# Two blocks on one core: projections of two pairs of heads moved beside linear and sparse attention, and another order of the first block's modulation

## The reference

```
mod_lat = silu(c) @ w_ada[l] + b_ada[l]          # 6 * 1024 columns, also for the context
h = rms_norm(x, g_mix) * (1 + sc1) + sh1
x = x + gt1 * mixer(h);  x = x + gt2 * conv_ffn(rms_norm(x, g_ffn) * (1 + sc2) + sh2)
```

```
h = rms_norm(x);  proj = h @ w_in   # qa ka va | qi ki wi | qb kb vb rb gl | uc
qa, ka, qi, ki = partial_rope(...)
o_a = sparse attention: per query the 128 best keys by the index scores, 8 heads of 64
o_b = gated linear attention of 4 heads, normalised, times silu(rb)
o_c = multi-scale pooling of uc
x = x + concat(o_a, o_b, o_c) @ w_out;  x = x + conv_glu_ffn(rms_norm(x))
```

## Time and profile before

| | us |
|---|---|
| median of 3 runs | 3632.78 (3628.01 to 3633.86) |
| profiled execution | 3633.83, its span 3632.0 |
| PE busy | 3459.5 (95%) |
| DVE busy | 2102.3 (58%) |
| ACT busy | 1321.1 (36%) |
| POOL busy | 121.8 (3%) |

### The profile page before, as it was taken

The page is one execution under the profiler, slowest core; times in us unless marked ns, Lnnn a source line. Parts: engine busy times, 40 slices in busy tenths (PEclk is TensorE's granted clock), DMA queues, the critical chain, the costliest instruction groups (busy, mean ns, idle before and its releaser), DMA issues.

```text
span 3632.0 us, 45947 instructions
## 1 busy us (share of the span) xinstructions
PE 3459.5 (95%) x18168; PEld 2771.1 (76%) x18168; DVE 2102.3 (58%) x3295; ACT 1321.1 (36%) x2084; POOL 121.8 (3%) x70
## 2 busy tenths in 40 slices
PE   6999999989999989999998999998999999899998
PEld 4866778878888877667777888775788877578887
DVE  4854663455575575445546664694566449646643
ACT  3344353333213323444433333344323234532322
POOL 0000000000000000000000000240000006000000
PEclk9999999999999999999999999998999999889999
DMA  5410202212261232101132333220232332013332
GB/s 231 150 41 13 86 25 87 64 49 62 99 220 60 96 124 69 41 18 47 54 95 78 93 95 104 91 83 7 83 96 93 102 99 82 30 58 97 94 98 93
DMA packets 79221, 300.56 MB, mean 83 GB/s; under 512 B 8784, under 2 KB 8912, under 8 KB 77904
## 3 DMA queue, kind: packets, MB, share of 16 engines
q1 hardware_dynamic: 77760, 291.47, 25.3%
q10 hardware_dynamic: 1296, 6.82, 0.5%
HBM read 296.16 MB, written 2.10 MB: 82 GB/s over the span
## 4 chain that ended last, share of the span: by engine, by line
PE 82%; DVE 11%; ACT 3%; DMA 2%; issue 2%; SPq 0%; DVEq 0%; ACTq 0%
PE ps L651 22%; PE ps L653 22%; PE ps L652 22%; PE ps L969 2%; DVE work L2716 2%; DVE top L2715 2%; PE ps L1011 2%; PE ps L1016 1%; PE ps L1039 1%; PE ps L1025 1%; PE ps L1046 1%; DVE ps L2187 1%; DVE ada_o L2187 1%; PE ps L706 1%; ACT split L1421 1%
## 5 line engine op out<-in xcount | busy, mean ns | idle before, releaser
L2009 DVE TENSOR_TENSOR split<-raw,split 128x1024 fp32r<-128x1024 f32 x412 | 504.4, 1224 | 821.6 <-ACT split L1421 820.7
L1421 ACT ACTIVATE split<-raw 128x1024 fp32r<-128x1024 f32 x442 | 466.5, 1056 | 756.3 <-PE ps L653 670.0
L651 PE MATMUL ps<-h,split 128*128 128x512 f32 x1328 | 532.5, 401 | 9.3 <-DVE split L2009 5.7
L653 PE MATMUL ps<-h,split 128*128 128x512 f32 x1328 | 525.3, 396 | 0.0
L652 PE MATMUL ps<-h,split 128*128 128x512 f32 x1328 | 525.2, 396 | 0.0
L651 PE MATMUL ps<-h_hl,split 128*128 128x512 f32 (+1 forms) x776 | 296.3, 382 | 19.3 <-DVE h_hl L2081 13.8
L651 PEld LDWEIGHTS ps<-h,split 128*128 128x128 f32 x1328 | 250.8, 189 | 75.8 <-issue 8.9
L652 PEld LDWEIGHTS ps<-h,split 128*128 128x128 f32 x1328 | 250.8, 189 | 60.7 <-issue 2.9
L653 PEld LDWEIGHTS ps<-h,split 128*128 128x128 f32 x1328 | 250.6, 189 | 59.4
L653 PE MATMUL ps<-h_hl,split 128*128 128x512 f32 (+1 forms) x776 | 279.4, 360 | 0.0
L652 PE MATMUL ps<-h_hl,split 128*128 128x512 f32 (+1 forms) x776 | 279.0, 359 | 0.0
(11 more groups left out here) (408 smaller groups left out, 6305.3 us busy)
## 6 DMA issues: line engine op xcount, KB each, us to landing
raw<-wstream SPq DMA_DIRECT2D x442, 512.0 KB, 3.5
ada_t<-ada_w SPq DMA_DIRECT2D x80, 512.0 KB, 4.8
first_w<-ada_first SPq DMA_DIRECT2D x4, 2048.0 KB, 25.6
x<-x_in SPq DMA_DIRECT2D x1, 3072.0 KB, 13.4
x<-x_in ACTq DMA_DIRECT2D x1, 3072.0 KB, 11.0
ada_c<-c_in SPq DMA_DIRECT2D x2, 1024.0 KB, 4.9
out<-x SPq DMA_DIRECT2D x8, 256.0 KB, 2.2
par<-params SPq DMA_DIRECT2D x1, 1345.0 KB, 6.6
```

The costliest lines, as they stand in the source:

```text
L651: nc.tensor.matmul(o, wh, a[0], start=first, stop=False)
L653: return nc.tensor.matmul(o, wl, a[0], start=False, stop=last)
L1421: nc.scalar.activation(split[:, n % SPLIT_SLOTS, 0, :], raw[:, n % RAW_SLOTS, :], copy).then_inc(hi_split, 1)
L2009: nc.vector.tensor_tensor(split[:, n % SPLIT_SLOTS, 1, :], raw[:, n % RAW_SLOTS, :], split[:, n % SPLIT_SLOTS, 0, :].bitcast(F32), ALU.sub ...
```

## The change

*First block.* PE's order at the start becomes modulation 0, sums of the norm, pick 0, modulation 2, spread, pick 2, modulation 1; modulation 3 comes before chunk 1, pick 1 before chunk 2, pick 3 before chunk 3. The two tiles of `ADA_AFTER[10]` are reduced before the low part of slab 10 instead of behind it. In both down projections the tiles are dealt over seven splits instead of nine, with the bias and the gains behind the eighth slab closed.

*Second block.* The slabs' order becomes qa 0, ka 0, qa 1, ka 1, ... Only pairs 0 and 1 are projected in `in2`; two decays go behind the first projection and one behind each of the next three events, and DVE makes two `decayed` behind the first rope and one behind each other. qa 2 is projected between `products(0)` and `products(1)`, ka 2 behind `products(1)`, both in bank 6. qa 3 and ka 3 are projected in bank 7 in pieces of one chunk (three matmuls) beside steps 0 to 7 of `dsa`, in two places of a step, before the values and before the transposes; their rotations stand in steps 4 and 8. All value tiles go to the two halves of bank 6. `mix` is eight buffers instead of one, since its old place is that of the activations `h2`, which now live on.

```diff
+ADA_AHEAD = LORA_SLABS + H_B
...
+IN2_ROPED = roped([((name, m), LAT, True) for m in range(2) for name in ("qa", "ka")])
+INDEX_ROTS, IN2_ROTS = 3, 3 + 4
+LATE_PAIR, LAST_PAIR = 2, 3
+
+def late_pieces(i):
+    if i < 4:
+        return [[("gemm", ("qa", LAST_PAIR), 2 * i)], [("gemm", ("qa", LAST_PAIR), 2 * i + 1)]]
+    if i == 4:
+        return [[("rot", ("qa", LAST_PAIR), 0)], [("gemm", ("ka", LAST_PAIR), 0), ("gemm", ("ka", LAST_PAIR), 1)]]
+    if i < 8:
+        return [[("gemm", ("ka", LAST_PAIR), 2 * i - 8)], [("gemm", ("ka", LAST_PAIR), 2 * i - 7)]]
+    return [[("rot", ("ka", LAST_PAIR), 0)] if i == 8 else [], []]
...
@@ SP, loads of tiles
-                        upto = ADA_SLOTS[group] + tiles * max(g - ahead - RAW_SLOTS, 0) // (BOTH_DOWN - 2)
+                        upto = ADA_SLOTS[group] + tiles * max(g - ahead - RAW_SLOTS, 0) // (BOTH_DOWN - 4)
@@ PE, first_two and mla(0)
+                    if 1 <= k <= len(beside):
+                        beside[k - 1]()
...
                     modulation(0)
                     tiles = norm_sums([(DC, BOTH)], sumN)
+                    pick(0)
                     modulation(2)
-                    pick(0)
                     norm_spread(0, tiles)
                     pick(2)
-                    beside = (lambda: (modulation(1), modulation(3)), lambda: (pick(1), pick(3)))
+                    modulation(1)
+                    beside = (lambda: modulation(3), lambda: pick(1), lambda: pick(3))
@@ PE, gla
                 products(0)
+                gemm(open_slab(), 0, DC, whole, (0, SEQ), True, bank=6)
                 pe.wait_ge(att_off, pairs.now() + 1)
                 pe.wait_ge(att_masked, pairs.now() + 1)
                 products(1)
                 pairs.add(2)
+                rotate("perm_2", qa[:, LATE_PAIR, :], owner[6], bank=7)
+                gemm(open_slab(), 0, DC, whole, (0, SEQ), True, bank=6)
@@ PE, dsa
+                rotate("perm_2", ka[:, LATE_PAIR, :], owner[6], bank=7)
...
                     if i + 2 < n:
                         scores(i + 2)
+                    if i == 0:
+                        pe.wait_ge(o_taken, outs.now())
+                    fill(i, 0)
                     if i:
                         value(i - 1)
+                    fill(i, 1)
                     turn_maps(i)
@@ ACT
-                projections(IN2_ROPED, INDEX_ROTS, beside=lambda j: decays(j - INDEX_ROTS))
+                projections(IN2_ROPED, INDEX_ROTS, beside=((0, 1), (2,), (3,), (4,)))
...
+                    for kind, name in late_ends(i):
+                        late_rot() if kind == "rot" else late_tile(name)
                     act.wait_ge(t_ready, items.now() + i + 1)
@@ DVE, split_low
+                    if n == ADA_AHEAD:
+                        ada_tiles(1, sum(ADA_AFTER[j] for j in ADA_AFTER if j < n), ADA_AFTER[n])
                     dve.wait_ge(hi_split, n + 1)
@@ DVE, ffn_both
-                                end = len(ADA_GROUPS[group]) * closed // (BOTH_DOWN - 2)
+                                end = min(len(ADA_GROUPS[group]) * closed // (BOTH_DOWN - 4), len(ADA_GROUPS[group]))
@@ DVE, gate_beside
-                    if n == 1:
+                    if n == 0:
                         dve.wait_ge(qk_scaled, 2 * (l + 1))
-                    if 0 <= n - 1 < len(HALVES):
-                        decayed(n - 1)
+                        decayed(0)
+                    decayed(n + 1)
@@ DVE, dsa, end of step i
+                    if i == 0:
+                        res.add()
+                        late_rope(("ka", LATE_PAIR), res.now())
+                    for kind, name in late_ends(i):
+                        res.add()
+                        if kind == "rot":
+                            late_rope(name, res.now())
+                        else:
+                            split_low()
```

More of the change, by code:

```diff
@@ L290, with late_ends @@
              + plain(("rb", 0), ("rb", 1)) + [("gate", "z", None)])
[L291 to L292 removed]
+IN2_ROPED = roped([((name, m), LAT, True) for m in range(2) for name in ("qa", "ka")])
[9 more added lines that the diff above has]
+    return [[("rot", ("ka", LAST_PAIR), 0)] if i == 8 else [], []]
+def late_ends(i):
+    return [(kind, name) for part in late_pieces(i) for kind, name, k in part if kind == "rot" or k == DC - 1]
 STEPS_2 = [(j, t) for j in range(HEADS // 2) for t in range(QT)]
@@ L798, in project @@
                     before = res.n
-                    first_two(first, act(names[0]), *beside)
+                    first_two(first, act(names[0]), beside)
                     at = {names[0]: before + len(first[0]), names[1]: res.n}
@@ L1283, in products @@
                     mm.then_inc(att_ready, 1)
+                whole = lambda k, g: own(h2)(k, (0, SEQ))
                 products(0)
+                gemm(open_slab(), 0, DC, whole, (0, SEQ), True, bank=6)
                 pe.wait_ge(att_off, pairs.now() + 1)
@@ L1304, in dsa, with fill @@
             def dsa(l):
-                wait_rot()
                 n = len(STEPS_2)
+                late = {"qa": qa, "ka": ka}
+                at = {}
                 pe.wait_ge(att_off, pairs.now())
                 pe.wait_ge(att_masked, pairs.now())
+                def fill(i, part):
+                    for kind, name, k in late_pieces(i)[part]:
+                        if kind == "rot":
+                            rotate("perm_2", late[name[0]][:, name[1], :], owner[7], bank=7)
+                            continue
+                        if k == 0:
+                            at["w"], at["o"] = open_slab(), open_acc(SEQ, 7)
+                        mm = product(at["o"], at["w"], k, own(h2)(k, (0, SEQ)), k == 0, k == DC - 1)
+                        if k == DC - 1:
+                            mm.then_inc(slab_used, 1)
                 def scores(i):
                     j, t = STEPS_2[i]
+                    if t == 0 and j != 1:
+                        rots.add(2 if j else 0)
+                        wait_rot()
                     if i >= 2:
@@ L1843, in gemm, with projections @@
                         bring(dsts[name[0]][:, name[1], :], o, closes=True)
-                def projections(events, j, beside=None):
+                def projections(events, j, beside=()):
+                    beside = list(beside)
                     for kind, name, g in events:
@@ L1864, in projections @@
                             bring(rot2[j % 2][:, :], o)
-                            if beside is not None:
-                                beside(j)
                             j += 1
+                        if beside:
+                            decays(*beside.pop(0))
                 projections(IN2_INDEX[:1], 0)
@@ L1908, in mix_high, with late_tile, late_rot @@
             def mix_high(k):
-                nc.scalar.activation(mix_hl[k][:, 0, :], mix[:, k, :], copy).then_inc(hi_ready, 1)
+                nc.scalar.activation(mix_hl[k][:, 0, :], mix[k][:, :], copy).then_inc(hi_ready, 1)
+            def late_tile(name):
+                kind, j = name
+                bank = 6 if j == LATE_PAIR else 7
+                o = take(SEQ, True, bank)
+                if kind == "qa":
+                    bring(qa[:, j, :], o, closes=True, scale=-HD ** -0.5)
+                else:
+                    bring(ka[:, j, :], o, closes=True)
+            def late_rot():
+                o, k = take(SEQ, False, 7), lates.n
+                lates.add()
+                if k % 4 >= 2:
+                    act.wait_ge(rot_done, rots.now() + k % 4 - 1)
+                bring(rot3[k % 2][:, :], o)
+            lates = Count()
             def gla(l):
                 for c in range(2):
-                    bring(mix[:, 6 + c, :], take(SEQ, False), ACT.Identity, scale=col(f"pool_scale{l}", c))
+                    bring(mix[6 + c][:, :], take(SEQ, False), ACT.Identity, scale=col(f"pool_scale{l}", c))
                 act.wait_ge(acc_taken, res.now())
@@ L1940, in high @@
                     mix_high(j)
+                late_rot()
                 exps(0)
@@ L1956, in dsa @@
                 high(n // QT - 1)
+                rots.add(4)
                 items.add(n)
@@ L2769, in gla, with late_rope @@
                     ins.then_inc(att_masked, 1)
+                    res.add()
+                    split_low()
+                    if p == 0:
+                        res.add()
+                    else:
+                        late_rope(("qa", LATE_PAIR), res.now(back=1))
+            def late_rope(name, taken):
+                kind, j = name
+                dst, k = (qa if kind == "qa" else ka)[:, j, :], lates.n
+                lates.add()
+                dve.wait_ge(acc_taken, taken)
+                rope(dst, rot3[k % 2][:, :], cos2[:, :], sin2[:, :]).then_inc(rot_done, 1)
+                rots.add()
+            lates = Count()
             def dsa(l):
@@ L3108, in weight_stream @@
         by_k(w, 2116, 256, 2)
-        for m in range(8):
```

(2 more changed lines are left out.)

59 lines of the change are left out of this document (33 added, 26 removed).

## The result

| | before | after |
|---|---|---|
| median of the runs, us | 3631.28 (6 runs, 3622.44 to 3635.35) | 3653.56 (6 runs, 3648.35 to 3656.91) |
| profiled execution, us | 3633.83, span 3632.0 | 3651.9, span 3650.1 |
| ratio | 1 | 1.0063, 95% interval 1.0049 to 1.0077 |

The account below looks back on a forecast made before the run. PE, busy 95% of the span, was taken as the bound, its work constant. Terms -6 - 5 + 4 + 8.4 + 7 = +8.4 us on 3633.83 gave 3642.2, as a median 3641; range 3620 to 3656 (8 in 10).

Parts of the forecast that it names:

- Part 1: Start-up modulation: the new order fills PE's waits for weights and activations, so chunk 4 comes earlier; -6 us.
- If modulation 1 has PE at its fast level: Start-up: condition that modulation 1 brings PE to its fast level before chunk 0; the gain is then 6.8 us, not 4.8.
- Part 2: First latent norm: two tiles done before split 10 let the norm's scaling start 5 us earlier; -5 us, bounds -3 and -6.
- Part 3: Down projections, tiles in seven slots: the second one's last split and slab come later; +4 us, bounds 0 and +6.
- eats slack only: 0 (bound +1.5): First down projection: DVE waits for splits there, so the denser tiles cost 0 us, at most +1.5.
- Part 4: Second block with two late pairs: earlier linear attention, longer sparse attention; +8.4 us in layer 0, +7 in layer 1.
- Up to the scores: Second block, linear attention to first scores: of 15.9 us gained at its start, 5.7 us were to remain.
- Beside sparse attention: Second block, from the first transposes on: 14 late pieces, two rotations and DVE's late ropes add 13.7 us.
- Rival 3: Start-up gives nothing because weights of blocks 1 or 3 come late: +14 us, 3647; chance 0.13.
- Rival 1: Second block: late pieces are free, swallowed by PE's waits in sparse attention; each layer gains 5 us, 3616; chance 0.12.
- Rival 2: First block's gains and second block's losses cancel: layers +3 us each, tile dealing nothing, 3628; chance 0.25.
- Edits at nothing: Shared bank 6, first pieces behind bank 7's copies, slab order and output buffers cost nothing; shared bank at most 2 us.

Follow-up runs that it names:

- e3: Old kernel with only the second block's change (two pairs of heads projected late): 3654.24 us, ratio 1.0058.
- e2: Old kernel with only the down projections' tiles dealt over seven slots and the early bias: 3640.31 us, ratio 1.0016.
- e9: Old kernel plus new start-up order, two tiles before split 10, second down projection's tiles a slot sooner, low half a step later: 3593.45 us, ratio 0.9896.
- e4: Changed kernel with late projection qa2 moved ahead of PE's wait for the decayed tensors: 3641.55 us, ratio to the old kernel 1.0027.
- e7b: Changed kernel with DVE making the low half of a finished pair's output one step later: 3619.72 us, ratio to the old kernel 0.9961.
- e6b: Old kernel with DVE making the low half of a finished pair's output one step later: 3610.15 us, ratio 0.9936.
- e8b: Changed kernel with one pair of heads projected late instead of two: 3629.32 us, ratio to the old kernel 0.9992.
- e1: Old kernel with only the new start-up order and the two tiles ahead of split 10: 3621.22 us, ratio 0.9970.

## Why the forecast was right in sign and short in size, step by step

**Part 1, -6: the step was under-priced.** Measured -9.6 in the stage. From chunk 0 to chunk 4 are 15.87 us, 16.2 in the working. The miss is all ahead of chunk 0: 4.75 us earlier, 0.8 forecast. I counted the pick's 0.8 and let everything else keep its duration; but norm sums, picks and spreading ran at the fast level (1.50, 1.03, 1.60 instead of 2.72, 1.87, 2.91). So the first pick fitted whole into the wait for block 2's weights (1.7 us off the path), spreading and the second pick gave 1.3 and 0.8, modulation 2 0.4, and all of PE's work began 0.6 us sooner, which no edit explains. "If modulation 1 has PE at its fast level" was the case that came, and earlier than I looked for it. It is not all the order's doing: e3, with the old one, gained 3.8 there, and the sums, in front of which nothing was changed, took 1.50 us in e2 with the old order and 2.72 in e9 with the new one. Spreading took 1.6 to 2.6 us in the ten executions with the new order, and 2.91 in three of the four with the old.

**Part 2, -5: right.** Scaling was foretold at 143.8 less the start-up's gain: 143.8 - 9.6 = 134.2, measured 134.14. The stage gave 3.9 to 6.6 in ten executions, -6.4 in after; the spread is the clock behind the norm.

**Part 3, +4: right for the second half, by another way; wrong for the first.** Down 2 is +4.3. The wait on sumD was foretold at 4 and is 3.2. PE waits on splits were foretold and came, 6.6 us for 2.1. What I left out are its waits for residuals (0.9, 1.2, 3.3), which stood behind up to six products of tiles; and the last residuals, which I had late behind the tiles, found DVE idle. PE's down projection got 12.6 us longer where I had 9.9. For the first one "eats slack only: 0 (bound +1.5)" failed: +2.1, again with a wait on a residual (1.33). I had compared tiles with splits, and not with the residual behind them.

**Part 4, +8.4 and +7: mechanism right, size off; this is the step that failed.** Linear attention 15.2 and 14.2 us earlier (15.9); a wait of 8.3 and 8.5 on L2828 (6 to 10); both as foretold, though POOL hit twice and not once (4.3 us), the case that the working put 1 us later. Then two terms, here for layer 0:
- *Up to the scores* 5.7 us were to be left of 15.9, and 2.5 were. The slow start after the wait was put at 1.5 + 1.6; it is 2.8 for the products and 2.7 for the projection, since the low level held nearly 12 us. e4 shows that this is the wait's doing, and that the clock falls again behind it.
- *Beside sparse attention* +13.7 was foretold from the transposes on, and is 67.5 - 51.2 = 16.3. The working had PE's own work at +11.5 less 1.0 for a clock kept up, and its waits at +3.2 (4.7 new, 1.5 filled). Measured are +15.9 of busy time and +0.4 of standing still. The rope behind DVE's wait was seen, and its waits came (2.48, with 1.9 us of pieces in front of it, and 4.26 where 2.21 stood), but the pieces filled as much elsewhere. What was short is the price of the work: where PE is fast a piece keeps the next instruction back by 0.75 to 0.9 us and a rotation by 1.06, for 0.7 and some 0.9 in the working, and e7b less e6b, both at a high clock, has 14.3 us for the 14 pieces and two rotations. The clock fell a little, to 0.84, instead of rising.

Layer 1 repeats this: 14.2 earlier, +13.0 up to the scores, +15.0 to the sums, +13.7 for 7.

**The sum.** +8.4 against +17.9 in the stages: part 4 +12.1, part 3 +2.4, parts 1 and 2 -5.0. Two under-priced gains hid 5.0 of the 14.5 us by which losses were under-priced. That was luck: without it the time would have been some 3658.6, outside the range. Rival 3 (weights late) did not occur: no DMA stood before modulations 1 and 3. Rival 1 is out: "waits of 15.5 us on DVE alone" were in few places, as said against it. Rival 2 would have needed +3 a layer; only e8b, with one pair late, comes to that (+0.5 and +2.9).

**Edits at nothing.** The shared bank 6 cost two waits of 0.9 in all the trace (value tiles behind DVE's copy), 1.7 us as against a bound of 2. The first pieces and the order of slabs show no wait of their own.

## What to carry to other kernels

A wait that looks like the price of an engine's work can be the price of its order: before moving work beside a stage, look at what the engine in front of the wait is itself waiting for, here DVE for a half that nobody needed for long. One line moved by a step took 0.6% off the old kernel's time, as much as the whole change added. Work moved beside another stage is paid in full there unless it fills a wait: 14 pieces and two rotations took 12.4 and 14.1 us with that half out of the way, and filled some 1.5. In front, taking 25.7 us of PE's work away moved the start by 15.2 and 14.2, since DVE's list was the bound, and the slow restart behind the new wait took 5.5 of them back in layer 0. One pair moved was neither won nor lost, two were dearer. And spread work into slots by the idle time in them, not evenly: two tiles drawn into an idle slot gave 5.2 us, the dealing into slots that were full took 6.4 over both halves.

## What was not expected of the hardware

- A wait can cost twice: three waits of 2.2 us removed shortened layer 0's sparse attention by 8.4 us, 4.6 of them standing still; the granted clock over the stretch rose from 0.86 to 0.96 and PE's busy time for the same matmuls fell from 38.61 to 34.80 us. With the norm behind it layer 1 gained 13.4.
- Small products can be followed by the low level after a wait of only 1.6 us (6.26 us for what takes 3.46, in e4 behind 80 products of the same kind), while the same products 0.46 us behind a projection ran fast.
- Executions differ by up to 3.8 us in stages that their kernels share; in the rows looked at the clock falls at another place (0.91 or 1.00 from 160 to 180 in kernels with the same order there). The profiled execution of e1 was 4 us better against before's than its median was.
